# RG-LRU's first convolution tap on ScalarE, VectorE's other three a weight half later

## The reference, cut to what matters

```python
u = h @ w_in                                # 1024 -> 2 x 1536
xb, yb = u[..., :D_RNN], u[..., D_RNN:]
y = gelu(yb)
xc = causal_conv(xb, conv_w, width 4) + conv_b     # one filter of 4 taps per channel
r = sigmoid(blockwise(xc) @ w_ra + b_ra); i = sigmoid(blockwise(xc) @ w_ix + b_ix)
a = exp(-8 * r * softplus(-lam));  bx = sqrt(1 - a*a) * (i * xc)
h_t = a_t * h_{t-1} + bx_t                  # along time
return (h * y) @ w_out
```

## Time and profile before

| | |
|---|---|
| median of three runs | 1784.45 us |
| the profiled execution's own time | 1782.9 us |
| its span, first to last instruction | 1781.1 us |
| TensorE / VectorE / ScalarE / GpSimd busy in the span | 1735.3 / 1309.2 / 861.4 / 393.4 us |
| mean granted TensorE clock | 0.993 |
| the RG-LRU's loop, and its output projection | about 18 to 121 us, and 121 to 154 us |

### The profile page before, as it was taken

The page is one execution under the profiler, slowest core; times in us unless marked ns, Lnnn a source line. Parts: engine busy times, 40 slices in busy tenths (PEclk is TensorE's granted clock), DMA queues, the critical chain, the costliest instruction groups (busy, mean ns, idle before and its releaser), DMA issues.

```text
span 1781.1 us, 32626 instructions
## 1 busy us (share of the span) xinstructions
PE 1735.3 (97%) x13254; PEld 1635.4 (92%) x13254; DVE 1309.2 (74%) x1681; ACT 861.4 (48%) x1136; POOL 393.4 (22%) x415
## 2 busy tenths in 40 slices
PE   7989999999989999999999999999999999999999
PEld 6879998998878999889998989999999989989998
DVE  7898889888666888978866768666666665676664
ACT  5865444455554544444445245444444435554442
POOL 0322013417613311630013204001200036430000
PEclk9999999999999999999999999999999999999999
DMA  8236567555402687655555535555355635336561
GB/s 321 97 122 220 192 235 257 193 186 203 148 2 71 218 275 265 227 180 188 191 212 186 179 125 188 189 198 203 125 206 183 223 138 184 122 120 211 175 229 44
DMA packets 50235, 321.89 MB, mean 181 GB/s; under 512 B 7472, under 2 KB 8816, under 8 KB 20048
## 3 DMA queue, kind: packets, MB, share of 16 engines
q1 hardware_dynamic: 37584, 286.58, 45.4%
q0 software_dynamic: 11104, 31.72, 5.6%
q10 hardware_dynamic: 1440, 2.10, 0.3%
HBM read 309.16 MB, written 10.09 MB: 179 GB/s over the span
## 4 chain that ended last, share of the span: by engine, by line
PE 89%; DVE 7%; ACT 2%; issue 1%; POOL 0%; DMA 0%; ACTq 0%; DVEq 0%; POOLq 0%
PE bank L2170 18%; PE bank L2176 17%; PE bank L2171 17%; PE bank L2172 17%; PE bank L2177 9%; DVE w_lo L1366 3%; PE bank L2429 1%; PE bank L2605 1%; PE bank L2771 1%; PE bank L2723 1%; PE bank L2439 1%; PE bank L2411 1%; ACT w_hi L940 1%; PE bank L2412 1%; PE bank L2413 1%
## 5 line engine op out<-in xcount | busy, mean ns | idle before, releaser
L1366 DVE TENSOR_TENSOR w_lo<-raw,w_hi 128x1024 fp32r<-128x1024 f32 (+2 forms) x516 | 682.7, 1328 | 274.6 <-ACT w_hi L940 272.4
L940 ACT ACTIVATE w_hi<-raw 128x1024 fp32r<-128x1024 f32 (+2 forms) x516 | 562.7, 1097 | 608.0 <-PE bank L2172 361.3
L2170 PE MATMUL bank<-hg_hi,w_hi 128*128 128x256 f32 (+1 forms) x2672 | 761.2, 285 | 14.0 <-DVE hg_lo L1371 10.3
L2171 PE MATMUL bank<-hg_lo,w_hi 128*128 128x256 f32 (+1 forms) x2672 | 756.8, 283 | 0.0
L2172 PE MATMUL bank<-hg_hi,w_lo 128*128 128x256 f32 (+1 forms) x2672 | 756.8, 283 | 0.0
L2170 PEld LDWEIGHTS bank<-hg_hi,w_hi 128*128 128x128 f32 (+1 forms) x2672 | 511.1, 191 | 19.0 <-DVE w_lo L1366 13.7
L2171 PEld LDWEIGHTS bank<-hg_lo,w_hi 128*128 128x128 f32 (+1 forms) x2672 | 511.2, 191 | 0.2
L2172 PEld LDWEIGHTS bank<-hg_hi,w_lo 128*128 128x128 f32 (+1 forms) x2672 | 511.1, 191 | 0.0
L2176 PE MATMUL bank<-hid,w_hi 128*128 128x512 f32 x1056 | 372.9, 397 | 0.0
L2177 PE MATMUL bank<-hid,w_lo 128*128 128x256 f32 x1056 | 296.3, 281 | 0.0
L2176 PEld LDWEIGHTS bank<-hid,w_hi 128*128 128x128 f32 x1056 | 198.5, 188 | 48.2 <-issue 1.0
(11 more groups left out here) (416 smaller groups left out, 2050.9 us busy)
## 6 DMA issues: line engine op xcount, KB each, us to landing
raw<-in_w SPq DMA_DIRECT2D x186, 1024.0 KB, 4.8
raw<-in_w SPq DMA_DIRECT2D x48, 1408.0 KB, 6.0
raw<-in_q SPq DMA_DIRECT2D x14, 768.0 KB, 4.2
raw<-in_w SPq DMA_DIRECT2D x8, 768.0 KB, 4.1
b_rows<-in_s_b_rows POOLq DMA_DIRECT2D x8, 512.0 KB, 7.7
l_rows<-s_powers POOLq DMA_DIRECT2D x64, 64.0 KB, 9.0
s_ca<-cp_s POOLq DMA_DIRECT2D x8, 512.0 KB, 4.1
s_ba<-ba_s POOLq DMA_DIRECT2D x8, 512.0 KB, 7.3
```

What stands on the lines that cost most here:

```text
L940: act.activation(w_hi[s][:, 0:n], raw[r][:, c * n:(c + 1) * n], ACT.Copy).then_inc(hi_made, 1)
L1366: dve.tensor_tensor(w_lo[s][:, 0:n], raw[r][:, c * n:(c + 1) * n], w_hi[s][:, 0:n].bitcast(F32), ALU.subtract).then_inc(lo_made, 1)
L2170: pe.matmul(psum, w_hi_ap, x_hi_ap, start=first, stop=False, **kw)
L2171: pe.matmul(psum, w_hi_ap, x_lo_ap, start=False, stop=False, **kw)
```

## The change

ScalarE makes tap 0 with one instruction per tile, `xb` times the tap's weight per channel plus the bias per channel, at its steps j = 3, 5, 9 and 11, behind the split of half j+4. VectorE's convolution keeps taps 1 to 3 and moves from steps 3, 5, 9, 11 to 4, 6, 10, 12, where it waits for `tap_made`. The waits for `xb` and for the free `xc` slot move from VectorE to ScalarE.

```diff
-CONV_AT = (3, 5, 9, 11)
+TAP_AT = (3, 5, 9, 11)
+CONV_AT = (4, 6, 10, 12)
...
+        tap_made = sem("tap_made")
...
+                def first_tap(g):
+                    slot = GT * (g % 2)
+                    act.wait_ge(xb_made, (GT * g + GT + 1) // 2)
+                    if g >= 2:
+                        act.wait_ge(gates_done, g - 1)
+                        act.wait_ge(ix_made, 2 * g - 3)
+                    for q in range(GT):
+                        act.activation(xc[:, slot + q, :], xb[:, slot + q, 1:1 + T], ACT.Identity, bias=gain("conv_b", GT * g + q),
+                                       scale=gain("conv_0", GT * g + q)).then_inc(tap_made, 1)
...
                     if j == 0:
                         root(ph["norm"])
                         joint_scales()
+                    if j in TAP_AT:
+                        first_tap(TAP_AT.index(j))
                     if j in DECAYS_AT:
                         decays(DECAYS_AT.index(j))
...
                 def conv(g):
                     slot = GT * (g % 2)
-                    for j in range(4):
+                    dve.wait_ge(tap_made, GT * g + GT)
+                    for j in range(1, 4):
                         for q in range(GT):
                             m = GT * g + q
                             x = xb[:, slot + q, 1 + j:1 + j + T]
                             o = xc[:, slot + q, :]
-                            if j == 0:
-                                last = dve.tensor_scalar(o, x, gain("conv_0", m), gain("conv_b", m), ALU.mult, ALU.add)
-                            else:
-                                last = dve.scalar_tensor_tensor(o, x, gain(f"conv_{j}", m), o, ALU.mult, ALU.add)
+                            last = dve.scalar_tensor_tensor(o, x, gain(f"conv_{j}", m), o, ALU.mult, ALU.add)
...
                     if j in CONV_AT:
                         g = CONV_AT.index(j)
-                        dve.wait_ge(xb_made, (GT * g + GT + 1) // 2)
-                        if g >= 2:
-
-                            dve.wait_ge(gates_done, g - 1)
-                            dve.wait_ge(ix_made, 2 * g - 3)
                         conv(g)
```

## The result

The changed kernel took 1792.1 us (median of 8 runs, 1787.1 to 1793.37), the one before 1784.18 (8 runs, 1782.3 to 1785.97). The ratio is 1.0041, 95% interval 1.003 to 1.0052: slower by some 7.3 us by the ratio; the two medians differ by 7.9. The profiled execution's span went from 1781.1 to 1789.1 us.

The account below looks back on a forecast made before the run. TensorE (97% busy) waits at the loop's end for VectorE's last subtraction. Lateness of 0.9, 5.6, 1.1 and a second wait of 4.2 with its taps, less 4.45 and 1.4, made 7.0 us: 1791.4 us, range 1787.0 to 1795.5.

Parts of the forecast that it names:

- Step A: Convolutions 0 and 1: ScalarE's taps wait for `xb`, leaving ScalarE 0.9 us late and the fifth `xb` pair at 61.6.
- Step B: Tap of group 2: ScalarE waits 5.6 us for `xb`, and the sigmoids of group 1 start 7.6 us late.
- The tap: ScalarE's Identity instructions with scale and bias per channel: 1.31 us for three, 2.0 allowed from above.
- Step C: Tap of group 3: ScalarE waits for the sixth `xb` pair at 72.7; half 17's split ends at 76.1, 8.4 late.
- Step D: From 67.65 on, all of ScalarE's list shifts by 8.4 us; half 22's split ends at 104.3.
- Step E: Loop's end: VectorE's decay meets or misses GpSimd's last product; half 23's subtraction 6.1 or 7.6 us late, 7.0 taken.
- The last term of the sum: At the end of the loop, 1.4 us that VectorE saves, taken off the lateness.
- Table loads: At ScalarE's taps: none counted, as ScalarE stands waiting for `xb` long enough for one of 1.28 us.
- TensorE: Ahead of the third gate products it waits some 4 us, and has that slack, needing the recurrence only at the end.
- (1): VectorE, full from 56.16 to the end, loses 3.04 us of work: faster, 1781.4 us; chance 0.04.
- (2): No measurable change: tap of group 3 finds `xb` ready, waits of 4.45 us absorb most; 1787.5 us, chance 0.10.
- (3): More: three taps cost 2.0 us and TensorE's gate products run at the lower clock; +10.4, 1794.9 us, chance 0.10.

Follow-up runs that it names:

- e6: Changed kernel with tap 0 on ScalarE only for groups 0 and 1, groups 2 and 3 whole on VectorE; 1784.7 us, ratio 1.0002.
- e1: Kernel before with only VectorE's convolutions moved to steps 4, 6, 10 and 12, all four taps kept on VectorE; 1783.67 us, ratio 0.9998.
- e7: Changed kernel with tap 0 on ScalarE only for groups 2 and 3, convolutions at 3, 5, 10, 12; 1789.59 us, ratio 1.003.
- e4: Kernel before with convolutions at 4, 6, 10, 12 and ScalarE waiting for `xb` at 3, 5, 9, 11 without making taps; 1788.38 us, ratio 1.0022.
- e10: Changed kernel with only group 2's tap on ScalarE, at step 11, and convolutions at 3, 5, 10, 11; 1783.71 us, ratio 0.9997.
- e8: Changed kernel with only groups 2 and 3 tapped on ScalarE, their taps and convolutions at steps 11 and 12; 1786.67 us, ratio 1.0012.
- e2: Changed kernel with tap 0 and its bias left out of the computation, VectorE doing taps 1 to 3; 1782.07 us, ratio 0.9989.

## Why the prediction was right

Forecast 1791.4 us, measured 1792.1. Its steps, with 0.18 us taken off the changed kernel's rows for its later start:

- *Step A* said 0.9 us late, fifth `xb` pair at 61.6. It ended at 61.91 - 0.18 = 61.7. As a part of the loss it was right too: e6 against e1, and the changed kernel against e7, give it 1.0 us.
- *Step B* said a wait of 5.6 us and sigmoids 7.6 late. The wait was 5.66, the sigmoids 65.79 - 0.18 - 57.72 = 7.9 late. The 0.3 are the tap.
- *The tap* was undersized: 1.31 us from the Exp row for three, measured 1.59, single ones 583 to 601 ns. An Exp of the same shape with one operand per channel takes 496 ns in the kernel before, so the second operand costs some 90 ns. The estimate by the Trainium skill, ScalarE: Activation LUTs, section What ACT_TABLE_LOAD costs, was up to 1.57 us for three; the trace agrees with its upper end.

```profile
L1076 ACT ACTIVATE xc<-xb,vec x12: 583/588/601, 31.7 to 73.8; 128x256 f32<-128x256 f32 x12
```

- *Step C* said that half 17's split ends at 76.1, 8.4 late. It ended at 76.29 - 0.18 = 76.1, 8.5 late. The longer taps were made up by a shorter second wait (3.78, forecast 4.2), as VectorE's nine took 5.39 and not 5.7 us beside GpSimd.
- *Step D* said that this goes on whole: half 22's split starts 103.41 - 0.18 - 94.81 = 8.4 late.
- *Step E* said that the decay's second operation meets GpSimd's last product or just misses it. It began 10 ns ahead of it (106.67 against 106.68 us), and half 23's subtraction met it instead, 2.36 us long in place of 1.23. The last `rec`: forecast 7.0 late, measured 7.2. The subtraction began 6.1 us late, the first of the prediction's two cases (6.1 and 7.6), and was then held for 1.1 more. The prediction named such a meeting as possible, but gave it no figure and took the middle of the two cases: that 7.0 came so near is partly luck. (Half 23's split in the kernel before ended at 98.97 and not at 99.1 us, a slip of 0.1.)
- *The last term of the sum*, "1.4 that VectorE saves", has the right size, 1.2, and the wrong name. From the start of the last root to the end of the last `rec` the kernel before takes 23.60 us and the changed kernel 22.40, but so do e1 and e4 (22.39), where VectorE has all its taps and saves nothing. Before, GpSimd's product began 0.05 us ahead of the decay's first operation and held it for its whole length. In ten of the eleven runs, as in the changed kernel, both operations of the decay are begun ahead of the product, and it holds only half 23's subtraction, behind a wait. In e10 it holds the decay's second operation, and the stretch takes 22.71 us. That is why the table's last column is the one before it less 1.2 us (0.9 in e10). Rows of e1's VectorE, which answer to 98.15 to 101.40 in the earlier trace rows:

```profile
98.34 0.94 DVE L1639 SCALAR_TENSOR_TENSOR inv_s<-rec_s,r_odd 128x768 f32<-128x768 f32 x1
99.32 0.56 DVE L1640 TENSOR_SCALAR inv_s<-inv_s 128x768 f32<-128x768 f32 x1
100.30 2.37 DVE L1366 TENSOR_TENSOR w_lo<-raw,w_hi 128x1024 fp32r<-128x1024 f32 x1 [0.42 <-ACT w_hi L940]
```

- *Table loads* at the taps: none were counted, and there are none.
- *TensorE*: 4 us of wait ahead of the third gate products, measured 3.68, then the clock at 0.50 for 3 us. Both were swallowed, but not for the reason given. The prediction said that TensorE needs the recurrence only at the end, and its wait for the first `rec` is indeed there still (3.76 us). It left out that ScalarE's splits wait for TensorE, which leaves some 0.2 us of slack (e8). TensorE's 5.8 us of lateness at the end of these products did no harm only because ScalarE was 8.4 us late already.

Of the rivals, (1) fell by e2 and e4: leaving tap 0 out altogether is worth 2 us at most, and the condition wasn't met. (2) needed the tap of group 3 to find its `xb` ready; it waited 3.78 us. (3)'s size for the tap (2.0) didn't come, and its clock didn't reach the end.

## What to carry to other kernels

When an operation moves to another engine, look at which operand it waits for and what stands behind it in the new engine's list. If the engine that makes that operand itself waits for something behind the moved instruction, it is a ring. The price is then the wait and the moved work on top, less the waits that the engine had there before, however idle it looked by its busy share (48%). Waits ahead of the place where an engine becomes full are slack as long as the engine that ends them isn't made late itself, and waits behind it are time: find that place first, as 67.65 us was here. And before calling another engine's lateness harmless, look for whoever waits for what it frees: TensorE's slack of some 0.2 us was found only by e1, e6 and e8.

## What the runs showed of the hardware

A VectorE operation with two SBUF inputs that met a GpSimd product stood until that ended: weight subtractions too took 2.36 us instead of 1.23, which the earlier trace rows had shown for the decay. It isn't only operations with two: a tap with one such input is held in the earlier trace rows, and the decay's second operation took 2.09 us instead of 0.56 beside the product of 90.06 to 92.08 us in the kernel before. GpSimd, starting beside a VectorE operation, was held in turn (2.25 us instead of 1.86).

```profile
90.41 2.09 DVE L1640 TENSOR_SCALAR inv_s<-inv_s 128x768 f32<-128x768 f32 x1
```

TensorE's lower clock after a wait was not the same from one kernel to the next. After waits of 2.13 us (e8) and 3.68 us (changed kernel) the gate products ran at 0.50; after one of 3.39 us, in e7, they took 5.23 us with the clock at 1.00 (timeline of e7, and a window of its TensorE alone):

```profile
69.76 5.23 PE L2370 MATMUL bank<-xc,gate_w 128*64 128x256 f32 x36 [3.39 <-DVE xc L1640]
```

```profile
69.70:73.00 3.30, 3.24 (x26) 1.00 0.29 45
```

What decides that stays open.
